# An encoder layer on one core: small transposes, the first normalisation and the late sums rearranged

## What is computed

```python
mod = silu(c) @ ada_w + ada_b                      # 9 vectors of 1024 per request
sh1, sc1, g1, sh2, sc2, g2, sh3, sc3, g3 = split(mod, 9)
h = rmsnorm(x, ffn1_norm) * (1 + sc1) + sh1
x = x + 0.5 * g1 * ((silu(h @ wg) * (h @ wu)) @ wd)       # FFN1, inner width 2816
h = rmsnorm(x, mix_norm) * (1 + sc2) + sh2
x = x + g2 * (concat(window_attention(h), latent_attention(h)) @ w_out)
h = rmsnorm(x, ffn2_norm) * (1 + sc3) + sh3
x = x + 0.5 * g3 * ((silu(h @ wg2) * (h @ wu2)) @ wd2)    # FFN2
x = rmsnorm(x, final_norm)
```

## Time and profile before

| | |
|---|---|
| median of 3 runs | 3444.66 us (3443.74 to 3452.62) |
| profiled execution | 3454.49 us, span of the core 3452.7 us |
| PE busy | 3199.3 us, 93% of the span |
| DVE, ACT, POOL busy | 1466.4, 810.0, 517.5 us (42%, 23%, 15%) |
| granted TensorE clock, mean | 0.963 of full speed |
| DMA | 207.49 MB, 60 GB/s over the span |

### The profile page before, as it was taken

How to read it: one execution, slowest core, us unless ns; L and a number is a source line. 1 busy time by engine, 2 the same in 40 slices (tenths; PEclk the granted TensorE clock), 3 DMA queues, 4 the chain that set the end, 5 groups by cost and what they waited for, 6 DMA issues and landing times.

```text
span 3452.7 us, 38874 instructions
## 1 busy us (share of the span) xinstructions
PE 3199.3 (93%) x14017; PEld 2487.4 (72%) x14017; DVE 1466.4 (42%) x2515; ACT 810.0 (23%) x1422; POOL 517.5 (15%) x303
## 2 busy tenths in 40 slices
PE   7899999999999987877498999999999999999999
PEld 2677877778778866766254555678888888888887
DVE  2556566565662344666344333235232232222224
ACT  3311111111111134555243333333111111111112
POOL 1111011111111132221000000252111111111110
PEclk9999999999999998888699999999999999999999
DMA  6112122121221021333621222221110101101001
GB/s 233 37 48 64 46 73 62 47 67 42 73 62 31 31 75 44 97 94 99 147 60 37 62 57 69 78 86 49 31 37 30 30 25 35 36 30 36 30 31 80
DMA packets 268158, 207.49 MB, mean 60 GB/s; under 512 B 16827, under 2 KB 240942, under 8 KB 268078
## 3 DMA queue, kind: packets, MB, share of 16 engines
q1 hardware_dynamic: 268078, 206.41, 20.2%
HBM read 169.31 MB, written 37.06 MB: 60 GB/s over the span
## 4 chain that ended last, share of the span: by engine, by line
PE 51%; DVE 5%; issue 3%; ACT 2%; SPq 1%; DMA 1%; POOL 0%; DVEq 0%; ACTq 0%; POOLq 0%
PE PS L423 12%; PE PS L424 12%; PE PS L425 12%; PE PS L1367 6%; PE PS L1318 1%; PE PS L1352 1%; PE PS L1351 1%; PE PS L1353 1%; PE PS L1331 1%; DVE z_sq L1041 1%; DVE mbuf L1484 1%; PE PS L901 1%; PE PS L1308 1%; PE PS L904 1%; PE PS L1343 0%
## 5 line engine op out<-in xcount | busy, mean ns | idle before, releaser
L423 PE MATMUL PS<-H_hi,W_hi 128*128 128x512 f32 x2304 | 914.1, 397 | 4.2 <-POOL W_lo L1667 4.2
L424 PE MATMUL PS<-H_lo,W_hi 128*128 128x512 f32 x2304 | 905.1, 393 | 0.0
L425 PE MATMUL PS<-H_hi,W_lo 128*128 128x512 f32 x2304 | 904.6, 393 | 0.0
L417 POOL TENSOR_TENSOR W_lo<-raw,W_hi 128x1024 fp32r<-128x1024 f32 x132 | 316.9, 2407 | 1891.8 <-ACT W_hi L390 1891.8
L554 DVE SCALAR_TENSOR_TENSOR XT<-PS,mod,XT 128x512 f32<-128x512 f32 x528 | 395.6, 750 | 298.5 <-PE PS L425 298.3
L423 PEld LDWEIGHTS PS<-H_hi,W_hi 128*128 128x128 f32 x2304 | 438.4, 190 | 96.1 <-issue 6.0
L425 PEld LDWEIGHTS PS<-H_hi,W_lo 128*128 128x128 f32 x2304 | 437.7, 190 | 93.5
L424 PEld LDWEIGHTS PS<-H_lo,W_hi 128*128 128x128 f32 x2304 | 438.2, 190 | 91.5 <-issue 1.4
L542 DVE TENSOR_TENSOR PS<-hid_g,PS 128x512 f32<-128x512 f32 x132 | 91.9, 696 | 883.9 <-PE PS L425 875.0
L390 ACT ACTIVATE W_hi<-raw 128x1024 fp32r<-128x1024 f32 x132 | 137.3, 1055 | 1231.0 <-PE PS L425 1230.6
L423 PE MATMUL PS<-hid_hi,W_hi 128*128 128x512 f32 x1056 | 414.5, 393 | 5.3 <-DVE XT L554 3.8
(11 more groups left out here) (197 smaller groups left out, 3064.8 us busy)
## 6 DMA issues: line engine op xcount, KB each, us to landing
ada_r<-in_ada_w SPq DMA_DIRECT2D x192, 128.0 KB, 2.2
raw<-in_ffn_wg SPq DMA_DIRECT2D x44, 512.0 KB, 3.8
raw<-in_ffn_wu SPq DMA_DIRECT2D x44, 512.0 KB, 3.8
raw<-in_ffn_wd SPq DMA_DIRECT2D x44, 512.0 KB, 3.6
ada_w_sb<-in_ada_w SPq DMA_DIRECT2D x6, 2048.0 KB, 15.2
raw<-in_w_out SPq DMA_DIRECT2D x24, 512.0 KB, 4.1
scr_qb<-qT_st SPq DMA_DIRECT2D x24, 384.0 KB, 4.5
scr_kb<-kT_st SPq DMA_DIRECT2D x24, 384.0 KB, 5.7
```

The source lines that it names most:

```text
L417: pool.tensor_tensor(W_lo[:, n % WS, :], raw[:, n % RS, :], W_hi[:, n % WS, :].bitcast(F32), ALU.subtract).then_inc(w_ready, 1)
L423: pe.matmul(out, w_hi, m_hi, start=first, stop=False)
L424: pe.matmul(out, w_hi, m_lo, start=False, stop=False)
L425: return pe.matmul(out, w_lo, m_hi, start=False, stop=last)
```

## The change

- **Late sums:** `ADA_AT` becomes (1, 3, 4, 7, 8, 9): reductions 1 and 2 stand one group later on PE.
- **Squares' sums at the start:** POOL's `fold_up` adds pairs and then two pairs together, 6 adds a chunk; PE's `sums_first` has 2 matmuls a chunk.
- **First normalisation:** the even blocks k go as before. For the odd ones POOL multiplies x by rstd (`xr`, two slots), ACT applies scale and shift twice, once rounded into `H_hi` and once in place into `xr`, and DVE subtracts. POOL does its four of chunk 0 ahead of the first weight's subtraction, and those of chunks 1 and 2 behind the second's.
- **Order on ACT:** the casts of weights 0 and 1 go ahead of chunk 0, and the cast of weight 3 behind the Silu of (0, 2).
- **First round of FFN1:** gate and up groups of weights 0 and 1 go chunk by chunk: (0,0), (1,0), (0,1), (1,1), (0,2), (1,2). The gate rows' transposes, `ada_turn(4)` and `(5)`, stand behind these six, with a wait for both copied rows ahead of (1, 1), whose PSUM bank one of them used. The arithmetic on the gates (`first_gates`) moves behind the third product on DVE.
- **Places:** `ada_row`, `rstd`, `xr`, `x_sq`, `xn`, `rows` get places of their own around the hidden tiles; FFN2's normalisation uses another buffer, `xn2`, of the same shape.

```diff
@@ -55,7 +55,7 @@
-ADA_AT = (1, 2, 3, 7, 8, 9)
+ADA_AT = (1, 3, 4, 7, 8, 9)
...
@@ -156,6 +149,11 @@
+        ada_row, = placed(HW + 32768, [("ada_row", [2, 2, CH], F32)])
+        rstd, xr = placed(HW + 39936, [("rstd", [P, NCH, CH], F32), ("xr", [P, 2, CH], F32)])
+        x_sq, = placed(HW + 50176, [("x_sq", [P, 4, CH], F32)])
+        xn2, = placed(HW + 32768, [("xn2", [P, 2, CH], F32)])
+        xn, rows = placed(HW + 56320, [("xn", [P, 2, CH], F32), ("rows", [P, P], F32)])
...
@@ -311,8 +310,13 @@
+        def first_round(f, it):
+            return f == 0 and isinstance(it, int) and it == 0
+
         def gu_order(f, it):
+            if first_round(f, it):
+                return [(n, c) for c in range(NCH) for n in range(2)] + [(n, c) for n in (2, 3) for c in range(NCH)]
             if f == 1 and isinstance(it, int) and it == 0:
...
@@ -413,6 +417,9 @@
             def body(it, ada):
                 for n in range(UNITS):
+                    if first_round(f, it) and n == 2:
+                        apply_pool_first(pool, 1)
+                        apply_pool_first(pool, 2)
                     pool.wait_ge(w_hi_ready, it * UNITS + (base + n + 1))
...
@@ -446,12 +453,17 @@
                     pe.wait_ge((silu_done, hid_ready)[role], it * 6 + (f * FT * NCH + t * NCH + c + 1))
+                    if first_round(f, it) and (n, c) == (1, 1):
+                        pe.wait_ge(ada_kept, 6)
...
                     mm.then_inc(ffn_steps, 1)
+                    if first_round(f, it) and (n, c) == (1, NCH - 1):
+                        ada_turn(pe, 4)
+                        ada_turn(pe, 5)
                     if ada and n * NCH + c in ADA_AT:
                         ada_reduce(pe, it, ADA_AT.index(n * NCH + c))
...
@@ -485,25 +497,32 @@
...
                 for n in range(4):
-                    if n == 3 or not isinstance(it, int) or it > 0:
+                    if n == 3 and not first_round(f, it) or not isinstance(it, int) or it > 0:
                         ffn_split_hi(act, f, it, n)
...
+                            hid_silu(act, f, it, t, c)
+                        if first_round(f, it) and t == 0 and c == 2:
+                            ffn_split_hi(act, 0, 0, 3)
...
@@ -545,6 +564,8 @@
+                        if first_round(f, it) and i == NCH - 1:
+                            first_gates(dve)
                 if f == 0 and last_round(it):
...
@@ -618,6 +639,22 @@
+        def fold_up(pool, c):
+            for h in range(2):
+                for p in range(2 * h, 2 * h + 2):
+                    pool.wait_ge(sq_ready, c * KD + 2 * p + 2)
+                    pool.tensor_tensor(sq_slot(c, 2 * p), sq_slot(c, 2 * p), sq_slot(c, 2 * p + 1), ALU.add) \
+                        .then_inc((sq_paired, sq_second)[p % 2], 1)
+                pool.wait_ge(sq_paired, c * NPP + 2 * h + 1)
+                pool.wait_ge(sq_second, 2 * c + h + 1)
+                pool.tensor_tensor(sq_slot(c, 4 * h), sq_slot(c, 4 * h), sq_slot(c, 4 * h + 2), ALU.add).then_inc(sq_paired, 1)
+
+        def sums_first(pe, c):
+            pe.wait_ge(root_ready, c + 1)
+            for h in range(2):
+                pe.wait_ge(sq_paired, c * NPP + 2 * h + 2)
+                pe.matmul(PS[:, 6, :], ones[:, :], sq_slot(c, 4 * h), start=(h == 0), stop=(h == 1)).then_inc(sq_used, 2)
+
...
@@ -638,10 +675,54 @@
...
+        def apply_pool_first(pool, c):
+
+            for k in range(1, KD, 2):
+                if c == 0 and k == 1:
+                    pool.wait_ge(rstd_ready, NCH)
+                if k >= 5 or c > 0:
+                    pool.wait_ge(h_ready, (c + 1) * KD + k - 3)
+                pool.tensor_tensor(xr[:, k // 2 % 2, :], XT[:, k, c * CH:(c + 1) * CH], rstd[:, c, :], ALU.mult) \
+                    .then_inc(xr_ready, 1)
+
+        def apply_act_first(act, c):
+            col = slice(c * CH, (c + 1) * CH)
+            for k in range(KD):
+                shift, scale = mod[:, SH1 * KD + k, c:c + 1], hscale[:, 0, k, c:c + 1]
+                n = c * (KD // 2) + k // 2 + 1
+                if k % 2 == 0:
+                    act.wait_ge(xn_ready, n)
+                    act.activation(H_hi[:, k, col], xn[:, k // 2 % 2, :], ACT.Identity, bias=shift).then_inc(hi_ready, 1)
+                else:
+                    act.wait_ge(xr_ready, n)
+                    act.activation(H_hi[:, k, col], xr[:, k // 2 % 2, :], ACT.Identity, bias=shift, scale=scale)
+                    act.activation(xr[:, k // 2 % 2, :], xr[:, k // 2 % 2, :], ACT.Identity, bias=shift, scale=scale) \
+                       .then_inc(xr_done, 1)
+
+        def apply_dve_first(dve, c):
+            col = slice(c * CH, (c + 1) * CH)
+            dve.wait_ge(rstd_ready, c + 1)
+            for k in range(0, KD + 2, 2):
+                if k < KD:
+
+                    dve.wait_ge(h_ready, (c + 1) * KD + max(k - 3, 0))
+                    dve.scalar_tensor_tensor(out=xn[:, k // 2 % 2, :], in0=XT[:, k, col],
+                                             scalar=hscale[:, 0, k, c:c + 1], in1=rstd[:, c, :],
+                                             op0=ALU.mult, op1=ALU.mult).then_inc(xn_ready, 1)
+                if k > 0:
+                    j, n = k - 2, c * (KD // 2) + k // 2
+                    dve.wait_ge(hi_ready, n)
+                    dve.scalar_tensor_tensor(out=H_lo[:, j, col], in0=xn[:, j // 2 % 2, :],
+                                             scalar=mod[:, SH1 * KD + j, c:c + 1], in1=H_hi[:, j, col].bitcast(F32),
+                                             op0=ALU.add, op1=ALU.subtract).then_inc(h_ready, 1)
+                    dve.wait_ge(xr_done, n)
+                    dve.tensor_tensor(H_lo[:, j + 1, col], xr[:, j // 2 % 2, :], H_hi[:, j + 1, col].bitcast(F32),
+                                      ALU.subtract).then_inc(h_ready, 1)
...
@@ -731,19 +812,19 @@
             pe.transpose(PS[:, 4, 0:NROW], rows[0:NROW, :], ident[0:NROW, 0:NROW]).then_inc(par_psum, 1)
             x_turn(pe, 0)
             x_turn(pe, 1)
-            sums_pe(pe, 0, 0)
+            sums_first(pe, 0)
             x_turn(pe, 2)
             pe.wait_ge(silu_ready, 1)
             ada_block(pe, 0)
-            sums_pe(pe, 0, 1)
+            sums_first(pe, 1)
             ada_block(pe, 1)
             ada_turn(pe, 0)
-            sums_pe(pe, 0, 2)
+            sums_first(pe, 2)
             for b in range(2, 6):
                 ada_block(pe, b)
-                if b != 4:
+                if b < 4:
                     ada_turn(pe, b - 1)
-                if b % 2 == 1:
+                if b == 3:
                     ada_turn(pe, b)
 
         def x_keep(act, c):
@@ -780,18 +861,15 @@
             root_act(act, 0, 2)
             ada_keep(act, 2)
             ada_keep(act, 3)
-            act.wait_ge(mod_ready, 1)
-            for k in range(KD):
-                apply_act(act, 0, 0, k)
             act.wait_ge(x_turned, NT + 2)
             ffn_split_hi(act, 0, 0, 0)
             ffn_split_hi(act, 0, 0, 1)
+            act.wait_ge(mod_ready, 1)
+            apply_act_first(act, 0)
             ada_keep(act, 4)
-            for k in range(KD):
-                apply_act(act, 0, 1, k)
+            apply_act_first(act, 1)
             ada_keep(act, 5)
-            for k in range(KD):
-                apply_act(act, 0, 2, k)
+            apply_act_first(act, 2)
             ffn_split_hi(act, 0, 0, 2)
 
         def x_keep_dve(dve, c):
@@ -831,10 +909,13 @@
                                               in1=par[:, ROW_G:ROW_G + KD], op0=ALU.add, op1=ALU.mult)
             mm.then_inc(mod_ready, 1)
             dve.wait_ge(mod_ready, 1)
-            apply_dve(dve, 0, 0)
-            apply_dve(dve, 0, 1)
+            apply_dve_first(dve, 0)
+            apply_dve_first(dve, 1)
             dve.wait_ge(ada_used, 6)
-            apply_dve(dve, 0, 2)
+            apply_dve_first(dve, 2)
+
+        def first_gates(dve):
+
             dve.wait_ge(ada_turned, 6)
             out = PS[:, 6, 0:2 * ADA_FIRST].rearrange("p (j s) -> p j s", s=2)
             for c in range(NCH):
...
@@ -1842,7 +1919,8 @@
             start_counts(pool, "pool")
             pool.sem_inc(w_ready, RS)
             for c in range(NCH):
-                pair_up(pool, 0, c)
+                fold_up(pool, c)
+            apply_pool_first(pool, 0)
             ffn_split_lo(pool, 0)
             mix_weight_lo(pool)
             mix_pool(pool)
```

More of the change, by code:

```diff
@@ L110, in build @@
         ada_acc = sb(sW, "ada_acc", [P, 2, 2, P])
[L111 to L117, removed]
         s3 = ExitStack()
@@ L225, in build @@
         xn_ready = sem("xn_ready")
+        xr_ready, xr_done, sq_second = sem("xr_ready"), sem("xr_done"), sem("sq_second")
         hi_ready = sem("hi_ready")
@@ L486, in ffn_pe, with hid_silu, hid_high @@
             ffn_rounds(pe, f, body)
+        def hid_silu(act, f, it, t, c):
+            act.wait_ge(ffn_steps, gu_step(f, it, 2 * t, c))
```

(27 more changed lines are left out.)

## The result

| | median, us | runs |
|---|---|---|
| before | 3444.73 | 3443.74 to 3452.62, n = 4 |
| changed kernel | 3407.78 | 3406.42 to 3411.54, n = 4 |

The ratio is 0.989 with a 95% interval of 0.9872 to 0.9907: 37 us faster in these medians, where 48.1 were forecast and 3396.6 predicted; 3407.8 is 0.8 us beyond the upper end of the range that I had named (3382 to 3407). The profiled execution of the changed kernel took 3408.2 us (span 3406.4). The prediction had 3406.4 for an execution like the profiled one of before (3454.5), and the two profiled spans differ by 46.3 us. So the forecast of the difference between two traces was 2 us off, and that of the median 11 us. Two questions follow: where the time went by the trace, and why the medians show less.

A forecast was written before the change was run, and what follows sets the result against it. TensorE was taken as the bound, held by waits at the late column sums. 51.5 us saved there less 3.4 lost at the start is 48.1; from the median 3444.66 that gives 3396.6 us, range 3382 to 3407.

The forecast's parts named there:

- What bounds: Whole kernel: TensorE, busy 93% of the span, is the limit; only shortening its work or its gaps shortens the end.
- part 1: Eight FFN1 rounds: later sums remove TensorE's waits and the half-speed stretches behind them, 51.5 us saved.
- The lower end that I named: Eight FFN1 rounds: 30.5 us gained if the waits go but the clock doesn't come back.
- a loss of 10 us at the start: Start: worst bound, with one more half-speed stretch, 7 instead of 5.2 us in the sums, and 2 us of hand-overs.
- theory A: Posed for the repeat of before: the 10 us lie outside the change's reach, in the attention part's execution-dependent clock.
- Part 2: Squares' sums at the start: folding on POOL makes the blocks and the modulation vectors 10.9 us later.
- Part 3: First normalisation: DVE and POOL lock each other out, so chunks run in series, 16.9 us, then 13.3 each.
- Part 4: First six gate/up groups: chunk-by-chunk order lets the first start at 112.2 us; they end at 150.5 against 147.16.
- the loss of 3.4 forecast: Start: folded sums, divided normalisation and new group order together lose 3.4 us.
- (a): Start: three engines do run side by side or the clock holds in the sums; 3376 to 3387 us, chance 0.22.
- (b): FFN1 rounds: sum 1 late again; half the gain gone, 3422 us, chance 0.06; all gone, 3448 us, chance 0.03.
- (c): Eight FFN1 rounds: clock falls under unbroken work, slower; 3487 us at clock 0.90, chance 0.02.

The follow-up runs named there:

- late_only: The kernel before with only ADA_AT changed to (1, 3, 4, 7, 8, 9): 3408.75 us, against 3451.16 for before beside it.
- late_undone: The changed kernel with ADA_AT put back to (1, 2, 3, 7, 8, 9): 3451.70 us, against 3451.16 for before beside it.
- before_again: The kernel before, unchanged, timed and profiled once more: 3450.11 us, ratio 1.000 to before beside it.
- unfold: The changed kernel with the squares' sums as before (four POOL adds, four ones-matmuls a chunk): 3398.39 us, ratio 0.9854 to before.
- unfold_early: The changed kernel with the squares' sums as before and the first two weights cast and split earlier: 3396.08 us, ratio 0.9864 to before.
- early_split: The changed kernel with the first two weights cast and split earlier, ahead of the vectors: 3408.98 us, ratio 0.9894 to before.
- two_unfold_early: The changed kernel with squares' sums as before, early weight splits and first normalisation on DVE and ACT alone: 3391.92 us, in a second timing 3392.31.

## Why the prediction was right and wrong

- **What bounds, and part 1's mechanism: right.** Rounds of 101.4 us, no wait at the sums, clock 1.00; late_only and late_undone show that it carries the whole gain.
- **Part 1's size for the median: wrong.** The step that failed is "862.7 - 8 x 101.4 = 51.5 us" taken from one execution and then subtracted from the median of others. The price of a wait is not a constant: 51.7, 47.9 and 41.4 us for the eight rounds in three executions of the same order. The execution of 3454.5 us was a dear one, 9.8 us above the median; that its dear waits are a good part of the reason is likely from these three figures, but no execution near the median of 3444.7 was traced. Against its own time the sum held (3406.4 forecast, 3408.2 measured), in part by luck as said above. For part 1 alone it promised 51.5, where late_only measured 42.4 against 23 runs of before. The lower end that I named, 30.5, was the waits alone and wasn't used for the range; the range's upper end, 3407, came out next to the measured 3407.8 from a loss of 10 us at the start, which did not happen.
- **The rest of the gap** is in the baseline and behind the rounds. The median of before was 3444.7 from 4 runs, 3451.2 from 23, 3445.9 and 3443.2 from 9 each. Behind round 9 the traces take 2278.8 (before), 2279.1 (before_again), 2285.5 (late_undone), 2283.0 (changed), 2286.3 (late_only), 2278.0 and 2280.7 (the two of the fastest kernel) and 2283.0 to 2287.1 us (the other five), without an order that follows the edits. The traces do place these 9 us. From round 9's start to the first weight cast of the output projection behind the attention (line 1663) it is 1030.3 us in before and 1037.9 in late_only, which is all of their difference. In the same 600 us of that part, from 500 us behind round 9's start, the granted clock is 0.96 in before, 0.95 in the changed kernel and 0.94 in late_only:

```profile
1673.92:2273.92 600.00, 546.06 (x2267) 328.45 (x2268) 204.30 (x359) 226.44 (x403) 36.88 (x18) 0.96 0.27 70
...
1623.38:2223.38 600.00, 545.71 (x2251) 327.43 (x2252) 203.59 (x358) 224.68 (x401) 35.62 (x17) 0.95 0.27 69
...
1623.14:2223.14 600.00, 544.68 (x2237) 326.02 (x2238) 202.85 (x357) 223.62 (x400) 33.63 (x16) 0.94 0.27 69
```

So what I had called theory A is at work too, between executions other than the two of before. Why the clock differs there stays open.

- **Part 2: right in kind and size.** 10.9 us forecast, 11.4 between the traces (83.52 to 94.89), 10.4 by unfold, and 13.5 between unfold_early and early_split (82.95 to 96.47). That the clock would fall inside the sums, carried over from other rows, was so in chunks 1 and 2. Term by term: chunks 1 and 2, with the block behind each, cost 7.0 us (7.8 forecast), chunk 0 some 3.6 (3.1), and 0.8 stood already before POOL's first add (25.22 us against 24.42).
- **Part 3: right.** Chunks in series, not side by side: 16.2, 13.1 and 12.0 us measured against 16.9, 13.3 and 13.3. The last was dearer in the forecast because I charged it POOL's next work, which it doesn't have.
- **Part 4: right.** First group near 111 us (112.2), warm again sooner: half speed until about 114, where I took it as long as before. The last chunk is ready at 136.1 us instead of 138.8. Between them the two make up for the 2.2 us between the loss of 3.4 forecast and the 1.2 measured.
- **The rivals.** (a) fell: two_unfold_early against unfold_early shows the division as no gain. (b) and (c) fell: no wait came back, and the clock held 1.00 over 811 us without a gap. What I had not named among them is the one that the runs point to: that the waits removed cost less in other executions than in the one profiled.

## What to carry to other kernels

Subtract a trace's price only from that trace's own time, and before the price of a repeated wait goes into a median, look whether its occurrences are alike in a second execution: a wait with a margin of half a microsecond to another engine's work can have two prices. Where PE is the bound, a long gap cost more than itself here; fewer matmuls bought with a gap of 5 us among them were a loss. Before work is divided between DVE and POOL, ask what DVE reads: here DVE was left with 12 instructions a chunk instead of 16, and every multiplication of POOL's that fell beside them made one of them about 1.0 us longer, of POOL's own 1.25.

## What the runs showed of the hardware

- A wait of PE of 1.25 us left the granted clock at 1.00, one of 3.82 was followed by 0.50. Between them there is no sharp line in these traces: 1.40 us kept 1.00, 1.42 and 1.45 were followed by 0.50 (late_undone). The half-speed stretch behind waits of the same length differed: 3.5 us lost in the round of rows 4 (351.20 - 341.78 less 5.44 and 0.51), and on the mean of all eight 2.6. The Trainium skill, "TensorE: Matmul & The Clock Gate", section "Part 1: The HAM clock gate", says that the point of the change differs from run to run; these traces agree.
- DVE and POOL take turns, instruction by instruction: 2.83 us for a 0.69 us subtraction beside a split of 2.4, 1.74 beside a multiplication, and POOL's own two splits 5.54 us, where twice the mean of rows 9 is 4.81. "SBUF — State Buffer" of the Trainium skill, cited in the prediction, holds at these rows.
- Not every DVE instruction is held up: in the trace of before its additions into `XT` (line 554), which take one operand from PSUM, keep their 0.75 us in all 20 cases that lie wholly inside a weight split of POOL (line 417). Reading a single tensor from SBUF was no protection: beside a split a product with a column (line 406) took 2.50 us instead of 0.28 (before_again, 338.55 us).
- This exclusion also sets the late sums' wait: 4.51 or 6.60 us for the same 14 instructions of DVE, by half a microsecond in their start; the last one alone makes the difference (0.35 or 2.43 us).
